# Two-layer decoder trunk with product-key experts: half the values' block and two query pairs of layer 1 are loaded once for both token chunks, and chunk 1 takes its expert heads in the order 4 to 7, 0 to 3

## The reference, cut to what matters

```python
q = (xc @ w_query).reshape(C, 8, 2, 128)              # 8 heads, 2 halves of a key
s = jnp.einsum('chpd,hpnd->chpn', q, subkeys)         # 128 scores for each half
...                                                   # top 16 of the sums: 16 experts a head
gate = jax.nn.softmax(top_s, axis=-1)
act = gelu(jnp.einsum('chkd,cd->chk', u_tbl[idx], xc))
coef = gate * act
return jnp.einsum('chk,chkd->cd', coef, v_tbl[idx])   # one row of u and one of v for each expert
```

## Time and profile before

| | before |
|---|---|
| median of 3 runs | 1741.36 us (1736.94 to 1742.15) |
| the profiled execution | 1739.16 us, of which the profile's span 1737.4 us |
| PE busy | 1429.9 us (82%) |
| DVE busy | 980.8 us (56%) |
| POOL busy | 975.1 us (56%) |
| ACT busy | 384.2 us (22%) |
| read from memory | 609.26 MB, 351 GB/s over the span |
| gathers (queue q0) | 536.94 MB, 81.7% of the 16 DMA engines' span |
| loads by SP (queue q1) | 73.44 MB, 12.2% of the 16 DMA engines' span |

### The profile page before, as it was taken

One profiled execution on the slowest core, in us unless ns is written; L12 is line 12 of the kernel. 1 busy time (PEld: TensorE's weight loads), 2 busy tenths in 40 slices (PEclk: granted clock), 3 DMA queues, 4 the chain that ended last, 5 costly groups with the idle time before them and its releaser, 6 DMA issues.

```text
span 1737.4 us, 17834 instructions
## 1 busy us (share of the span) xinstructions
PE 1429.9 (82%) x5137; PEld 821.8 (47%) x5137; DVE 980.8 (56%) x2411; ACT 384.2 (22%) x900; POOL 975.1 (56%) x1038
## 2 busy tenths in 40 slices
PE   8988889798887987979798797998979778766766
PEld 8975645354344544434454455545445443222322
DVE  2266466465665563566745634745665665565654
ACT  1111222112211222232322222322222222111211
POOL 0054556666565646566656555464656656666663
PEclk9998999798897989989899898898989979888887
DMA  9489999999998999999999999897999989999997
GB/s 319 143 282 328 340 349 357 375 351 381 370 361 331 352 400 372 394 408 408 395 342 402 350 367 390 320 377 263 365 406 364 361 326 331 373 357 374 353 368 274
DMA packets 199500, 611.30 MB, mean 352 GB/s; under 512 B 17596, under 2 KB 50436, under 8 KB 199428
## 3 DMA queue, kind: packets, MB, share of 16 engines
q0 software_dynamic: 147456, 536.94, 81.7%
q1 hardware_dynamic: 51972, 73.44, 12.2%
HBM read 609.26 MB, written 1.05 MB: 351 GB/s over the span
## 4 chain that ended last, share of the span: by engine, by line
PE 50%; issue 18%; DVE 11%; DMA 7%; POOL 6%; another core or an unknown queue 5%; ACT 2%; POOLq 1%; SPq 0%; DVEq 0%; ACTq 0%
PE sums L743 31%; PE banks L641 8%; PE banks L656 6%; DMA rows<-in_peer_u,expert 5%; DVE rows L1395 5%; POOL rows L591 3%; POOL rows L579 3%; DMA rows<-in_peer_v,expert 2%; PE banks L665 1%; PE sums L648 1%; PE banks L786 1%; PE banks L719 1%; DVE find L1346 1%; DVE side_i L1351 0%
## 5 line engine op out<-in xcount | busy, mean ns | idle before, releaser
L743 PE MATMUL sums<-rows,soft_diag 128*128 128x512 f32 x2032 | 971.9, 638 | 163.8 <-issue 108.7
L591 POOL DMA_INDIRECT rows<-in_peer_v,expert x512 | 486.1, 949 | 495.3 <-PE sums L743 319.2
L743 PEld LDWEIGHTS sums<-rows,soft_diag 128*128 128x128 f32 x2032 | 411.3, 206 | 693.0 <-issue 658.4
L1395 DVE SCALAR_TENSOR_TENSOR rows<-rows,xn_near 128x1024 f32<-128x1024 f32 x512 | 605.8, 1218 | 229.5 <-DMA rows<-in_peer_u,expert 155.6
L579 POOL DMA_INDIRECT rows<-in_peer_u,expert x512 | 486.8, 951 | 250.5 <-issue 242.6
L1059 ACT ACTIVATE soft_diag<-ident,coef 128x128 f32<-128x128 f32 x508 | 158.5, 389 | 61.0 <-PE sums L743 26.4
L1051 ACT ACTIVATE gelu<-dots 128x8 f32<-128x8 f32 (+1 forms) x65 | 13.4, 207 | 494.6 <-issue 242.0
L1463 DVE SCALAR_TENSOR_TENSOR spare<-banks,soft_diag 128x512 f32<-128x512 f32 (+1 forms) x8 | 7.7, 958 | 160.6 <-ACT soft_diag L1084 160.6
L641 PE MATMUL banks<-xT,wring 128*128 128x128 f32 x640 | 84.6, 289 | 15.9 <-issue 14.4
L641 PEld LDWEIGHTS banks<-xT,wring 128*128 128x128 f32 x640 | 79.9, 203 | 21.7 <-issue 20.3
L1005 ACT ACTIVATE scores<-banks 128x256 f32<-128x256 f32 (+1 forms) x46 | 21.2, 464 | 304.4 <-remote 104.8
(11 more groups left out here) (138 smaller groups left out, 957.2 us busy)
## 6 DMA issues: line engine op xcount, KB each, us to landing
wring<-in_w_kv SPq DMA_DIRECT2D x16, 1024.0 KB
wring<-in_peer_w_query SPq DMA_DIRECT2D x11, 1024.0 KB
wkept<-in_peer_w_query SPq DMA_DIRECT2D x10, 1024.0 KB
rows<-in_peer_u,expert POOLq DMA_INDIRECT x512
rows<-in_peer_v,expert POOLq DMA_INDIRECT x512
wring<-in_attn_w_q SPq DMA_DIRECT2D x8, 1024.0 KB
rows<-in_conv_w_in SPq DMA_DIRECT2D x7, 1024.0 KB, 11.9
wkept<-in_conv_w_out SPq DMA_DIRECT2D x4, 1024.0 KB
```

What stands on the lines that cost most here:

```text
L591: pool.indirect_dma_start(v_row[j], None, v_table, bass.IndirectOffsetOnAxis(ap=expert[b][:, k:k + 1], axis=0)).then_inc(v_landed[j], 16)
L743: last = nc.tensor.matmul(sums[:, half, :], diag[:, k % GROUP, :], v_row[k % V_SLOTS][:, half * 512:(half + 1) * 512], start=(first and k ...
L1395: nc.vector.scalar_tensor_tensor(out=u_row[j], in0=u_row[j], scalar=1.0, in1=xn_near[:, :, :].rearrange("p a d -> p (a d)"), op0=ALU.mult, ...
```

## The change

Chunk 0's block of values for heads 8 to 15 stays in two `wring` buffers until chunk 1 has used it, so chunk 1 takes values' half 1 first and half 0 after. Query pairs 2 and 3 are loaded once: chunk 1 takes its pairs in the order 2, 3, 0, 1 (`PAIR_ORDER`), so that it uses pair 2 and pair 3 in slots 12 and 14, while the copies made for chunk 0 are still there. Pair (0, 2), which chunk 0 needs from step 20 on, moves on PE from the end of slot 0 to the end of slot 5, its `score_pair` from slot 1 to ahead of slot 6's `combine`. Two more places take loads for part of the time: `XT`, the buffer of the normed transposed chunk (`xT`), and `SOFT`, half of the buffer that attention's weights use, for which that buffer and `spare` become one. SP gets a second wait on three loads (`ALSO`). In all, SP issues four loads of 1 MB less.

```diff
+    PAIR_ORDER = ((0, 1, 2, 3), (2, 3, 0, 1))
...
+    stream_values(0, 1, (1, 2), 1)
+    stream_whole(peer_subkeys[1], None, ("subkeys", 1, 3), "subkeys", 1)
+    placed([XT], "subkeys", 1)
...
+    stream_pair(0, 0, (0, XT), (0, 0))
+    stream_qry(1, SOFT)
+    stream_pair(0, 1, (0, XT), (0, 1))
+    stream_key(1, 0)
     for kh in range(2):
-        BLOCK["queries", 1, 3, kh] = BLOCK["queries", 0, 3, kh]
+        BLOCK["values", 1, 1, kh] = BLOCK["values", 0, 1, kh]
+    stream_key1(1, 0)
+    stream_values(1, 0, (1, 2), 1)
+    stream_qry1(1, 0)
+    stream_keys(1, (1, 2))
+    stream_qrys(1, 0, 0)
+    stream_pair(0, 2, (1, 2), (1, 0))
+    stream_qrys(1, 1, 0)
+    stream_pair(0, 3, (0, XT), (1, 1))
+    for at in range(2):
+        for kh in range(2):
+            BLOCK["queries", 1, at, kh] = BLOCK["queries", 0, 2 + at, kh]
+    for at in range(2, 4):
+        stream_pair(1, at, KEEPS[2 * at - 4:2 * at - 2], (1, at))
+
+    ALSO = {BLOCK["subkeys", 1]: FILL["values", 0, 1], BLOCK["qry", 1, 0]: FILL["heads", 0, 3],
+            BLOCK["queries", 0, 3, 1]: FILL["qrys", 1]}
...
+                if m in ALSO:
+                    sp.wait_ge(bank_done, ALSO[m] + 1)
...
-                    else:
-                        query_pair(0, 2)
                     transpose_norm("kv", c)
...
-                    if c == 1:
-                        score_pair(0, 2)
...
+                else:
+                    if t == 3:
+                        first_half(half_to_tokens, kvT, "values", c, 0)
+                        second_half(half_to_tokens, kvT, "values", c, 0)
+                        to_features(take("qry", c, 1), weights_of("qry", c, 1), mixT, P)
+                    if t == 4:
+                        wait_read(pe, "values", c, 0)
+                        heads_out(c, 0)
+                        wait_read(pe, "qry", c, 1)
+                        logits(c, 1)
+                        first_half(half_to_features, kvT, "keys", c)
+                        second_half(half_to_features, kvT, "keys", c)
+                    if t == 5:
+                        first_half(half_to_features, mixT, "qrys", c)
+                        query_pair(0, 2)
+                    if t == 6:
+                        second_half(half_to_features, mixT, "qrys", c)
+                        heads_out(c, 1)
+                        wait_read(pe, "qrys", c)
+                        logits(c, 2)
...
+                    if c == 1 and t == 6:
+                        score_pair(0, 2)
                     combine(n, n % 2, t % GROUPS)
                     mixer_slot(c, t)
...
-                if c == 1 and t == 2:
+                if c == 1 and t == 6:
                     pair_scored(0, 2)
...
+                if t == 5 and c == 1:
+                    pair_queried(0, 2)
```

More of the change, by code:

```diff
@@ L267, in trunk, with placed @@
         stream_whole(peer_w_query[0], hd * COLS, ("query", 0, 1, hd), "query", 0, hd)
-    def stream_pair(c, m, last=None):
-        stream_halves(peer_w_query[1], 2 * m * COLS, ("queries", c if last is None else last, m), "queries", c, m)
-    for c in range(CH):
-        if c == 1:
-            stream_pair(0, 2)
+    PLACE = {}
+    XT, SOFT = W_RING + W_EARLY + W_KEPT + 4, W_RING + W_EARLY + W_KEPT + 5
+    KEEPS = [W_RING + W_EARLY + i for i in range(W_KEPT)]
+    def placed(slots, *name):
+        for kh, slot in enumerate(slots):
+            PLACE[BLOCK[(*name, kh) if len(slots) > 1 else name]] = slot
@@ L282, in trunk @@
-        stream_halves(attn_w_q[0], 2 * COLS, ("qrys", c), "qrys", c)
-        stream_halves(w_kv, D + 2 * COLS, ("values", c, 1), "values", c, 1)
-        if c == 0:
-            stream_whole(peer_subkeys[1], None, ("subkeys", 1, 3), "subkeys", 1)
-            for j in range(NB - 1):
-                stream(attn_w_o[0], (2 * j, 2), 0, ("half", HALF["out", 1, j]), "out", j)
-            stream(attn_w_o[0], (2 * NB - 2, 2), 0, ("bank", FILL["out", 1, 1]), "out", NB - 1)
-        else:
-            stream_pair(0, 3, last=1)
@@ L291, in trunk, with stream_values, stream_keys @@
-        for m in range(2):
-            stream_pair(c, m)
-    stream_pair(1, 2)
-    for kh in range(2):
-        BLOCK["queries", 1, 3, kh] = BLOCK["queries", 0, 3, kh]
+        placed([slot], "qry", c, 1)
+    def stream_values(c, half, slots, last):
+        stream_halves(w_kv, D + 2 * half * COLS, ("values", last, half), "values", c, half)
+        placed(slots, "values", c, half)
+    def stream_keys(c, slots):
+        stream_halves(w_kv, 2 * COLS, ("keys", c), "keys", c)
+        placed(slots, "keys", c)
@@ new lines, in stream_qrys, with stream_pair @@
+    def stream_qrys(c, kh, slot):
+        k = kh * KT // 2
+        stream(attn_w_q[0], (k, KT // 2), 2 * COLS, ("bank", FILL["qrys", c]) if kh else ("half", HALF["qrys", c]), "qrys", c, kh)
+        PLACE[BLOCK["qrys", c, kh]] = slot
+    def stream_pair(c, at, slots, last):
+        stream_halves(peer_w_query[1], 2 * PAIR_ORDER[c][at] * COLS, ("queries", *last), "queries", c, at)
+        placed(slots, "queries", c, at)
+    stream_key(0, 0)
+    stream_qry(0, 1)
+    stream_values(0, 0, (2, 0), 0)
@@ new lines, in trunk @@
+    stream_key1(0, 1)
+    stream_qry1(0, 2)
+    stream_keys(0, (0, 1))
+    stream_qrys(0, 0, 2)
+    stream_qrys(0, 1, 0)
+    stream_values(0, 1, (1, 2), 1)
+    stream_whole(peer_subkeys[1], None, ("subkeys", 1, 3), "subkeys", 1)
+    placed([XT], "subkeys", 1)
+    for j in range(NB):
+        stream(attn_w_o[0], (2 * j, 2), 0, ("half", HALF["out", 1, j]) if j < NB - 1 else ("bank", FILL["out", 1, 1]), "out", j)
+        placed([KEEPS[j]], "out", j)
+    stream_pair(0, 0, (0, XT), (0, 0))
@@ L301, in trunk @@
     assert len(EARLY_SLOTS) == BLOCK["query", 0, HEADS - 1] + 1 and W_RING == 3 and KEPT == 11
[L302 to L310 removed]
+    w_slot = EARLY_SLOTS + [PLACE[m] for m in range(len(EARLY_SLOTS), len(blocks))]
     def before_in_slot(m):
@@ L1161, in mixer_slot @@
                     heads_made(c, 1)
-                if t == 8:
+                if t == 8 and c == 0:
                     values_made(c, 1)
```

140 lines of the change are left out of this document (78 added, 62 removed).

## The result

The changed kernel takes 1749.3 us (median of 20 runs, 1744.42 to 1755.96), the kernel before 1741.34 us (20 runs, 1736.94 to 1752.51). The ratio is 1.0035 with a 95% interval of 1.0019 to 1.0051: slower by 0.35%, some 6 us (the two medians lie 8.0 us apart). The time lies outside the range of the prediction, by 1.3 us, and on the other side of its forecast. The profiled execution took 1745.22 us with a span of 1743.5 us, 6.1 us more than the span before. That is near the measured loss, but each profile is one execution: a second profile of the kernel before, taken later in another session, has a span of 1747.5 us. So a slot that differs by a few microseconds between two profiles is a hint, and no more until other profiles show it too.

What follows compares the result with a forecast made beforehand. DMA engines and PE's work outside `combine` were taken to bound the stretch by turns. Slots 15 to 7 gave +2.5 us, two later loads -5.8, together -3.3: from 1741.4 to 1738 us, range 1729 to 1748 us.

Steps and rivals of the forecast that it cites:

- The step that failed: Slot 0: the pair leaves with its gaps, 16.2 us, and the gathers' 22.2 us then hold; 34 to 22, -12 us.
- The second step that failed: Slot 12 to step 24: two dropped loads, those for pair (1, 2), taken in full at 2.9 us each, -5.8 us.
- slot 15 (-3 for -2): Slot 15 of chunk 0: one load gone, POOL's gathers allow no less than 20 us; 23 to 21, -2 us.
- the "+4": End of slot 5: PE waits for ACT's read of the pair, then for diagonals behind its scores; +4 us.
- the 1.9: Slot 6: PE's `heads_out` waits for ACT's read of `qrys` and the attention weights, 1.9 us with handovers.
- slot 5 was to grow by 12.5: Slot 5: half of `qrys` leaves (-3.6), pair (+7.2) and scores (+0.9) come, gaps +4, ACT waits +4; +12.5 us.
- where I had 6.7: Slot 5: gaps in its run of 116 small matmuls, 4 us added to today's 2.7.
- the 103 of the forecast: Slots 4 to 6 together: 103 us against 82 before.
- the +2.5 us foretold for slots 15 to 7: Chunk 0's slot 15 through slot 7: time given back in slots 15 and 0 is spent again in slots 4 to 6.
- The second rival: Slots 4 to 6 become too long, gaps growing with the run of small matmuls: +10 us, 1751 us; chance 0.20.
- The first rival: All four loads count; gaps come from crowded DMA engines or program place, not run length: 1730 us; chance 0.36.
- Its other half: First rival, on small matmuls: gaps don't come from run length, so slot 5 gets no 4 us, slot 6 no 3.5.

Runs made afterwards that it cites:

- both ACT edits: Changed kernel; ACT makes slot 6's diagonals and attention weights ahead of its reads there, and reads other pairs' scores behind the diagonals: ratio 1.0003.
- the two kernels with the pair in slot 0 and ACT's order mended: Kernel before, and the changed kernel with pair (0, 2) back in slots 0 and 1; ACT reads pairs' scores behind the diagonals: ratios 0.9985 (0.9993 again) and 0.9981.

## Why the prediction was wrong

**The step that failed is slot 0**: "PE would need under 18 us, so the gathers' 22.2 us hold: 22, that is -12". PE did need 17.6 us, but the slot took 33. The gaps of the earlier trace rows were real in that execution, but I took them as the pair's price in every one, and I set only PE and the gathers against each other. The next bound under the pair was DVE's chain: search for experts, `xn`, eight dot products, coefficients. In both kernels the coefficients came 10.2 us behind `xn`. With slot 1 together 13 us were foretold and 6 came; the runs put what the pair's work was worth in slot 0 at some 4 us (0.9972, for three quarters of it). The slots to which the pair went had no such cover, and PE paid there. One profile does have slot 0 at 22.4 us, the changed kernel with both ACT edits: its search took 9.0 us. Its next `combine` began at 966.0 us all the same, where the two kernels with the pair in slot 0 and ACT's order mended have 967.2 and 966.2 on the same chip.

**The second step that failed**: "I take them in full: 2 x 2.9 = -5.8 us". The stretch of slot 12 to step 24 became 3 us longer instead. The share of 0.99 that I took as the sign of a bound is no such sign: with four loads cut it is 0.96 in that stretch and the stretch 128 us long, with twenty cut it is 0.91 and the stretch 130. The 132 of the changed kernel are probably no effect of the change: its other three profiles, with edits in slot 5 and in ACT's order, have 129 to 130 there, and the kernel before has 128.0 and 130.4 in its two, from `combine` to `combine`. So dropping the two loads gained nothing there that a profile or a time shows.

**Right were** slot 15 (-3 for -2), slot 3 (-1 for -0.5), and the mechanism of the waits in slots 5 and 6: 0.78 and 3.10 us for the "+4", 1.71 for the 1.9. PE did not wait for a weight load in slot 3, so the later values' half cost nothing there, and q1 carries 69.25 MB for 69.2. Slot 2 looks right with +2 for 0, but the profiles of the changed order have 31.6 to 36.0 us there and those of the kernel before and its variants with the old order 26.9 to 28.5: the gaps that stood in slot 1 stand in slot 2, and the 5 us that slot 1 seems to give back are in good part only moved.

**Of the right kind and the wrong size**: slot 5 was to grow by 12.5 and grew by 8, slot 4 by 3.5 and grew by 5, slot 6 by 5.5 and grew by 3. In slot 5 PE is busy for 31.4 of 38 us; the new waits leave 2.7 us of gaps where I had 6.7. So gaps don't grow with the run of small matmuls in this profile: slot 5 has the longest run and few, slot 4, with 96, has 7.3 us of idle PE. Slots 4 to 6 took 98 us, 5 less than the 103 of the forecast. That the +2.5 us foretold for slots 15 to 7 missed the +7 by no more than 4.5 us is luck: the forecast asked 11 us too much of slot 0, and this was offset by slots 4 to 6 (5 us) and slot 1 (4 us).

**The rivals.** The second rival (slower, 1751 us) has nearly the number and not the mechanism: it needed slots 4 to 6 above 112 us, and they took 98. The loss came from what slot 0 and the end did not give back. The first rival (all four loads count) is refuted by the two runs with cut loads. Its other half, that gaps have no price by the length of the run, holds: the same 64 pieces of the pair run in 7.3 us in five profiles and in 14.5 to 23.2 in three. The Trainium skill, "Runtime: NRT & Kernel Launch", section on instruction fetch mechanics, calls the cost of going on to the next block of instructions "mostly hidden", and the profiles agree as far as a long run has no price of its own. Whether the gaps are waits for instructions no run shows. What makes them stays open: in slot 8 they stand with twenty loads cut as without.

**The sum with the measured terms**: +7 in slots 15 to 7, -1 in slot 8, +1 to slot 12, +3 in the stretch from there, -3 before and -1 behind: +6 us. This is the sum of two single executions; that the loss is the move's rests on the run with the move alone, at a ratio of 1.0040. How the move's loss divides into the pair's matmuls in slot 5, ACT's waits and what slot 0 doesn't give back isn't settled: the runs that tried these parts differ by 0.1 to 0.4%, each uncertain by some 0.2%.

## What to carry to other kernels

Before you give a gap to the work around which it stands, follow the other engines' chain through the same stretch: work that lies under another engine's chain gives little back when it is taken out (here 4 us where 12 were foretold), and costs time where it is put into a slot that its own engine bounds. Profile the same kernel twice before you price a slot: slot 0 of one kernel took 34.5 us in one execution and 40.1 in another. A busy share of the DMA engines near 1.0 is no proof that bytes set the time; cut some loads to a few KB and look, ahead of rebuilding the buffers to save them. When work moves, move its reads on the other engines with an eye to what stands behind them there.

## What the runs showed of the hardware

- The DMA engines' busy share is a poor measure of load here: in the kernel before it was 0.99 from slot 12 to step 24, at 375 GB/s; with chunk 1's loads cut it was 0.91 at 336 GB/s there, and the stretch as long. These are shares in which loads and gathers lie together; whether the gathers alone bound the end of the kernel, where there are no loads, was not tried.
- The same search for experts takes very different times on DVE. In the changed kernel it took 21.9 us in slot 0 (928.35 to 950.27) and 8.9 us in slot 6 (1118.84 to 1127.78). In slot 0 of the changed kernel DVE stands four times for 1.94 to 3.18 us with no releaser on the core ("remote"), while POOL issues a gather every 1.24 us; in slot 6 POOL issues three in that time. DVE's timeline of slot 6 of the changed kernel, the first and last operation:

```profile
1118.84 0.29 DVE L1444 COPY find<-scores 128x256 f32<-128x256 f32 x1
...
1127.61 0.17 DVE L1471 TENSOR_SCALAR expert<-expert_f 128x16 uint32<-128x16 f32 x1
```

  In the kernel before, slot 0's search took 15.0 us (934.16 to 949.20). That suggests the gathers' issue as the cause, but one profile speaks against it as the whole one: in the changed kernel with both ACT edits the search in slot 0 took 9.0 us, while POOL issued eight gathers 1.23 to 1.34 us apart. No run here tried it. As slot 0's length hangs on it, it is the next thing to look at. The search's first and last operation in that profile:

```profile
942.98 0.29 DVE L1445 COPY find<-scores 128x256 f32<-128x256 f32 x1
...
951.76 0.17 DVE L1472 TENSOR_SCALAR expert<-expert_f 128x16 uint32<-128x16 f32 x1
```

- The idle gaps of 0.3 to 2.6 us inside runs of small matmuls come with loads or without, and not in every execution: query pair (0, 2) in slot 0 ran without one in five profiles and with gaps in three, in 22.6 us in the kernel before's second profile. Their cause is open.
